# First layer input transposed on the host, its first two weight blocks side by side; the last chunks tile by tile, with smaller stores

## What is computed

```python
h = rms_norm(x, norm_mix_pre)                 # 256 x 2048
proj = h @ w_in                               # 2048 x 10240: q, k, v of two attentions, gates
q, k = rope(q), rope(k); oa, on = two attentions
mixed = sig(ga) * (oa @ w_a) + sig(gb) * (on @ w_b)
x = x + rms_norm(mixed @ w_out, norm_mix_post)
x = x + rms_norm(relu(rms_norm(x) @ w_up)**2 @ w_down, norm_mlp_post)
proj = rmsnorm(x, norm_w_2) @ w_in_2          # mLSTM and HGRN2 parts
x = x + y @ w_out_2
x = x + sigmoid(rmsnorm(x, pe_norm_w_2) @ w_pg) * (p @ w_pe)
out = rmsnorm(x, final_norm_w)
```

## Time and profile before

| | us |
|---|---|
| median of three runs (2017.31 to 2017.79) | 2017.42 |
| the profiled execution, its own time | 2017.24 |
| its span in the profile | 2015.5 |
| TensorE busy | 1992.3 (99%) |
| VectorE busy | 1175.5 (58%) |
| ScalarE busy | 981.9 (49%) |
| mean granted clock of TensorE | 0.997 |

### The profile page before, as it was taken

One profiled execution on the slowest core, in us unless ns is written; L12 is line 12 of the kernel. 1 busy time (PEld: TensorE's weight loads), 2 busy tenths in 40 slices (PEclk: granted clock), 3 DMA queues, 4 the chain that ended last, 5 costly groups with the idle time before them and its releaser, 6 DMA issues.

```text
span 2015.5 us, 22345 instructions
## 1 busy us (share of the span) xinstructions
PE 1992.3 (99%) x9256; PEld 1655.0 (82%) x9256; DVE 1175.5 (58%) x1075; ACT 981.9 (49%) x956; POOL 40.6 (2%) x42
## 2 busy tenths in 40 slices
PE   8999999999999999999999999999999999999997
PEld 6888888888888888888888888888898888888786
DVE  6645546645656644443356666677387858675554
ACT  5345544545445444444455555554556445454443
POOL 0000000000000000000000000000000000230000
PEclk9999999999999999999999999999999999999999
DMA  7564555555657356666655555564556444355442
GB/s 252 195 202 144 161 190 181 181 183 192 209 188 251 119 178 184 187 188 188 185 180 199 189 189 198 197 229 168 167 161 199 163 146 163 130 209 203 157 167 105
DMA packets 184894, 366.79 MB, mean 182 GB/s; under 512 B 6616, under 2 KB 13400, under 8 KB 184152
## 3 DMA queue, kind: packets, MB, share of 16 engines
q1 hardware_dynamic: 184792, 365.36, 55.1%
HBM read 363.24 MB, written 2.10 MB: 181 GB/s over the span
## 4 chain that ended last, share of the span: by engine, by line
PE 95%; ACT 2%; DVE 1%; issue 1%; DMA 0%; SPq 0%; POOL 0%; DVEq 0%; ACTq 0%
PE acc L1325 89%; PE mis L1325 4%; PE mis L1328 2%; ACT hi L480 1%; DVE m L844 1%; DMA raw<-in_w_in 0%; ACT ath L497 0%; DVE atl L887 0%; DVE lo L862 0%; DVE xs L844 0%; SPq L334 0%; ACT m L470 0%; ACT m L469 0%; ACT spare L480 0%; DVE m L852 0%
## 5 line engine op out<-in xcount | busy, mean ns | idle before, releaser
L862 DVE TENSOR_TENSOR lo<-raw,hi 128x2048 fp32r<-128x2048 f32 (+1 forms) x333 | 754.9, 2269 | 645.4 <-ACT hi L480 643.1
L1325 PE MATMUL acc<-hi,ath 128*128 128x512 f32 (+1 forms) x2672 | 1050.0, 393 | 4.9 <-DVE atl L887 3.8
L1325 PE MATMUL acc<-hi,atl 128*128 128x512 f32 (+1 forms) x2672 | 1034.7, 387 | 0.0
L1325 PE MATMUL acc<-lo,ath 128*128 128x512 f32 (+1 forms) x2672 | 1033.4, 387 | 0.0
L480 ACT ACTIVATE hi<-raw 128x2048 fp32r<-128x2048 f32 (+1 forms) x333 | 628.8, 1890 | 380.6 <-PE acc L1325 374.5
L1325 PEld LDWEIGHTS acc<-hi,ath 128*128 128x128 f32 x2672 | 501.9, 188 | 105.6 <-issue 5.4
L1325 PEld LDWEIGHTS acc<-hi,atl 128*128 128x128 f32 x2672 | 501.5, 188 | 102.4
L1325 PEld LDWEIGHTS acc<-lo,ath 128*128 128x128 f32 x2672 | 502.1, 188 | 98.0 <-issue 0.5
L469 ACT ACTIVATE m<-mis 128x512 f32<-128x512 f32 (+1 forms) x96 | 50.3, 524 | 222.0 <-PE mis L1328 193.1
L469 ACT ACTIVATE m<-acc,st 128x512 f32<-128x512 f32 (+1 forms) x102 | 69.3, 679 | 117.0 <-PE acc L1325 116.2
L844 DVE TENSOR_TENSOR m<-m 128x512 f32<-128x512 f32 (+2 forms) x117 | 71.9, 615 | 22.8 <-ACT m L469 18.1
(11 more groups left out here) (113 smaller groups left out, 547.4 us busy)
## 6 DMA issues: line engine op xcount, KB each, us to landing
raw<-in_w_in SPq DMA_DIRECT2D x135, 1024.0 KB, 5.1
raw<-in_w_up SPq DMA_DIRECT2D x64, 1024.0 KB, 5.5
raw<-in_w_down SPq DMA_DIRECT2D x64, 1024.0 KB, 5.0
raw<-in_w_out SPq DMA_DIRECT2D x32, 1024.0 KB, 5.1
raw<-in_w_pg SPq DMA_DIRECT2D x16, 1024.0 KB, 5.1
raw<-in_w_in SPq DMA_DIRECT2D x12, 688.0 KB, 4.2
raw<-in_w_a SPq DMA_DIRECT2D x8, 1024.0 KB, 5.1
raw<-in_w_b SPq DMA_DIRECT2D x8, 1024.0 KB, 5.0
```

Of the source, the lines that this page charges most:

```text
L862: e.tensor_tensor(lo, raw, hi.bitcast(F32), ALU.subtract).then_inc(s_lo.on("lo", n))
L1325: return e.matmul(o, a, b, start=start, stop=stop)
```

## The change

x is also given transposed from the host, as `xt` (128 partitions x 16 contraction tiles x 256 tokens), and so is p2. `XT` takes 16 KB of each partition in a region that is free at the start. The three transposes of groups on TensorE and the multiply on DVE go: ACT makes `ath` of one contraction tile for both token tiles in one ACTIVATE whose scale is the norm weight (`x_high`), DVE `atl` in one scalar_tensor_tensor (`x_low`), each of 128 x 256.

Chunks 0 to 7 are renumbered: 0, 2, 4, 6 are block 0 and 1, 3, 5, 7 block 1, so two chunks use each group of x. Chunk 1 comes in four pieces too. `first()` on TensorE takes chunk 0 piece by piece for both token tiles. ACT issues four transfers itself (`cols` and group 0 of `xt` in three) and runs a Copy of 128 x 1 on a constant ahead of its first wait. The plain x, which the row means and the residual need, comes behind chunk 5. One `warm(20, 0)` takes the place of the two runs of 12. The level masks come as bytes and are not cast.

At the end, chunks 337 to 339 are computed for t = 0 and then for t = 1. `finish` works on the last block in halves of 256 columns, the mean is folded into the squares' scale and a constant column, and a tile's rows are scaled and stored in four pieces of 384, 384, 768 and 512 columns, the second of them issued by ACT.

```diff
+        XT = m(32, 4096).rearrange("p (k s) -> p k s", k=16)
...
-        for j in range(20):
+        for j in range(2):
+            blocks.append(("rope", j, 512, []))
+        for k in range(0, 16, 4):
+            for j in range(2):
+                blocks[j][3].append(len(chunks))
+                src = w_in[k * P:(k + 4) * P, 512 * j:512 * j + 512].rearrange("(k p) c -> p k c", p=P)
+                chunks.append((src, 512, j, k, 16, "x", k))
+        for j in range(2, 20):
             kind = "rope" if j < 4 else "va" if j < 6 else "hd" if j < 10 else "vn" if j < 12 else "gt"
             plan(kind, j, w_in, 0, 16, 512 * j, 512, "x")
...
-        for j in (0, 1, 2, 3, 6, 7, 8, 9):
+        for n, j, t in ((7, 0, 0), (7, 0, 1), (8, 1, 0), (9, 1, 1)):
+            beside(n, "heads", "rope", j, t)
+        for j in (2, 3, 6, 7, 8, 9):
             for t in range(2):
                 beside(4 * j + 4 + t, "heads", "rope" if j < 4 else "hd", j, t)
...
-        beside(308, "p", 0)
-        beside(310, "p", 1)
...
-        before[0, 0] = [("x", 0, 0), ("x", 0, 1)]
-        before[0, 1] = [("x", 1, 0), ("x", 1, 1)]
-        for g in range(2, 4):
-            for t in range(2):
-                before[g - 1, t] = [("x", g, t)]
+        for g in range(1, 4):
+            behind[2 * g - 2] = [("x", g, 0)]
...
-            load(XS[:, 0, 0:512], xv[:, 0, 0:512], "x", 0, 0)
-            load(IDN[:, :], id_c, "id")
-            load(COL[:, :], cols, "col")
-            for j in range(4):
-                load(RAW[0][:, 512 * j:512 * j + 512], w_in[j * P:(j + 1) * P, 0:512], "first", j)
-                if j == 0:
-                    load(XS[:, 1, 0:512], xv[:, 1, 0:512], "x", 0, 1)
+            for n in range(2):
+                for j in range(4):
+                    load(RAW[n][:, 512 * j:512 * j + 512], w_in[j * P:(j + 1) * P, 512 * n:512 * n + 512], "first", n, j)
+            raw(2)
             for g in range(1, 4):
-                if g < 3:
-                    raw(g)
-                load(XS[:, :, 512 * g:512 * g + 512], xv[:, :, 512 * g:512 * g + 512], "x", g)
+                load(XT[:, 4 * g:4 * g + 4, :], xt_[:, 4 * g:4 * g + 4, :], "xt", g)
+                raw(2 + g)
+            for t in range(2):
+                load(XS[:, t, :], xv[:, t, :], "x", t)
             load(COS, cos_c.rearrange("(t p) c -> p t c", p=P), "cos")
             load(SIN, sin_c.rearrange("(t p) c -> p t c", p=P), "sin")
+            raw(6)
+            load(IDN[:, :], id_c, "id")
+            load(LAMV, lamv.partition_broadcast(P), "lam")
+            raw(7)
             load(NAM, nam_c, "nam")
-            load(LAMV, lamv.partition_broadcast(P), "lam")
-            load(m(24, 1024).rearrange("p (n c) -> p n c", n=8), lvl_c, "lvl")
+            load(LVL[:, :, :], lvl_c, "lvl")
             load(CAU[:, :], caus_c, "cau")
             load(BIF[:, :], bif, "bif")
-            for n in order[3:]:
+            for n in order[8:]:
...
-                    load(PN, p2.rearrange("(t p) c -> p t c", p=P), "p")
+                    load(PTT, p2.rearrange("p (k s) -> p k s", k=2), "p")
...
             for t in range(2):
-                for c in range(2):
-                    o = slice(1024 * c, 1024 * c + 1024)
-                    if c == 0:
-                        sp.wait_ge(s_act, "out", t, c)
-                    else:
-                        sp.wait_ge(s_dve, "out", t, c)
-                    e.dma_start(o_d[:, t, o], XS[:, t, o]).then_inc(s_out.on("out", t, c), 16)
+                for c in (0, 2, 3):
+                    sp.wait_ge(*((s_act if c < 2 else s_dve), "out", t, c))
+                    e.dma_start(o_d[:, t, slice(*PIECES[c])], XS[:, t, slice(*PIECES[c])]).then_inc(s_out.on("out", t, c), 16)
             sp.wait_ge(s_out, LAST)
+            sp.wait_ge(s_out2, "out", 1)
...
+                if name == "x":
+                    ac.wait_ge(loaded("xt", g), "xt", g)
+                    for k in range(4 * g, 4 * g + 4):
+                        x_high(k)
+                    return
...
+            def x_high(k):
+                ac.wait_ge(loaded("col"), "col")
+                e.activation(ATH[:, k, :], XT[:, k, :], ACT.Copy, scale=COL[:, C_PRE + k:C_PRE + k + 1]).then_inc(
+                    s_ach.on("ath", "x", k))
...
             def finish(b):
-                ids = blocks[b][3]
                 for t in range(2):
-                    ac.wait_ge(s_prod, "products", ids[-1], t)
+                    ac.wait_ge(s_prod, "products", N_ALL - 1, t)
                     ac.wait_ge(s_dve, "gated", 2, t)
-                    act(SG[t], acc[:, 2 * (b % 2) + t, :], ACT.Sigmoid, scale=ST[:, 60 + t:61 + t]).then_inc(s_act.on("evac", b, t))
-                    if t == 1:
-                        out_rows(0)
-                    ac.wait_ge(s_dve, "gated", 3, t)
-                    act(JK2, XS[:, t, 1536:2048], ACT.Square, accum=ST[:, 43 + 4 * t:44 + 4 * t]).then_inc(s_act.on("out sq", 3, t))
-                out_rows(1)
-
-            def out_rows(t):
-                ac.wait_ge(s_pool, "row", N_ALL - 1, t)
-                ac.wait_ge(s_dve, "weighed", 1, t)
-                act(XS[:, t, 0:1024], XS[:, t, 0:1024], ACT.Copy, scale=ST[:, 48 + t:49 + t]).then_inc(s_act.on("out", t, 0))
-
-            do = dict(lam=lam, da=da, na=na, sig=sig, ut=ut, cut=cut, prep=prep, conv=conv, gate=gate, hg=hg, ml=ml, p=p)
+                    for h in range(2):
+                        o = slice(256 * h, 256 * h + 256)
+                        act(SG[t][:, o], acc[:, 2 * (b % 2) + t, o], ACT.Sigmoid, scale=ST[:, 60 + t:61 + t]).then_inc(
+                            s_act.on("last sigmoid", t, h))
+                    for h in range(2):
+                        ac.wait_ge(s_dve, "gated", 3, t, h)
+                        act(JK2[:, 0:256], XS[:, t, 1536 + 256 * h:1792 + 256 * h], ACT.Square, scale=D ** -0.5,
+                            accum=SUMS[t][:, 3 + h:4 + h]).then_inc(s_act.on("last sq", t, h))
+                    for c in range(2):
+                        o = slice(*PIECES[c])
+                        ac.wait_ge(s_pool, "row", N_ALL - 1, t)
+                        ac.wait_ge(s_dve, "weighed", 1, t)
+                        act(XS[:, t, o], XS[:, t, o], ACT.Copy, scale=ST[:, 48 + t:49 + t]).then_inc(s_act.on("out", t, c))
...
-            unit("x", 0, 0)
-            first(0)
-            unit("x", 0, 1)
-            for j in range(1, 4):
-                first(j)
-            high(1)
+            def first(n, j):
+                h, w = (z[n][:, 512 * j:512 * j + 512] for z in (HI, RAW))
+                ac.wait_ge(loaded("first", n, j), "first", n, j)
+                e.activation(h, w, ACT.Copy).then_inc(s_hi.on("hi first", n, j))
+
+            e.dma_start(COL[:, :], cols).then_inc(loaded("col").on("col"), 16)
+            for k, c in ((0, 1), (1, 1), (2, 2)):
+                e.dma_start(XT[:, k:k + c, :], xt_[:, k:k + c, :]).then_inc(loaded("xt", 0, k).on("xt", 0, k), 16)
+            ac.wait_ge(s_pool, "mhalf")
+            act(MHALF[:, 15:16], MHALF[:, 15:16], ACT.Copy).then_inc(s_act.on("table"))
+            for j in range(4):
+                ac.wait_ge(loaded("xt", 0, min(j, 2)), "xt", 0, min(j, 2))
+                x_high(j)
+                first(0, j)
+            for j in range(4):
+                first(1, j)
...
-                if n == 3:
+                if n == 4:
                     for t in range(2):
-                        for g in range(4):
-                            ac.wait_ge(loaded(*(("x", 0, t) if g == 0 else ("x", g))), *(("x", 0, t) if g == 0 else ("x", g)))
+                        ac.wait_ge(loaded("x", t), "x", t)
                         act(m(48, 2048), XS[:, t, :], ACT.Square, accum=ST[:, t:t + 1]).then_inc(s_act.on("x sq", t))
...
+            def x_low(k):
+                dv.wait_ge(s_ach, "ath", "x", k)
+                e.scalar_tensor_tensor(ATL[:, k, :], XT[:, k, :], COL[:, C_PRE + k:C_PRE + k + 1], ATH[:, k, :].bitcast(F32),
+                                       ALU.mult, ALU.subtract).then_inc(s_dve.on("atl", "x", k))
+
+            def first(n, j):
+                h, l, w = (z[n][:, 512 * j:512 * j + 512] for z in (HI, LO, RAW))
+                dv.wait_ge(s_hi, "hi first", n, j)
+                e.tensor_tensor(l, w, h.bitcast(F32), ALU.subtract).then_inc(s_lo.on(*(("lo first", n, j) if j < 3 else ("lo", n))))
...
             def finish(b):
-                gated(3, 0, b)
-                row_mean(N_ALL - 1, 0, None)
-                gated(3, 1, b)
-                weighed(3, 0)
-                row_mean(N_ALL - 1, 1, None)
-                out_rows(0)
-                weighed(3, 1)
-                out_rows(1)
+                for t in range(2):
+                    r = ST[:, 48 + t:49 + t]
+                    for h in range(2):
+                        x_, g_ = XS[:, t, 1536 + 256 * h:1792 + 256 * h], SG[t][:, 256 * h:256 * h + 256]
```

(52 more changed lines are left out.)

92 lines of the change are left out of this document (33 added, 59 removed).

## The result

Measured four times beside the kernel before, the changed kernel takes **2006.42 us** in the median (2006.01 to 2007.72) against 2017.39 (2017.31 to 2017.79): a ratio of 0.9946, with a 95% interval of 0.9929 to 0.9964. That is 11.0 us gained where 8.9 were forecast. The profiled execution took 2006.48, with a span of 2004.6 us.

The account below looks back on a forecast made before the run. TensorE, busy 1992.3 of 2015.5 us, was taken as the bound. Start 8.0 + p2 0.0 - chunk 338 0.1 + end 1.0 = 8.9 off 2017.24 gave 2008.3, median 2008.5; range 2004.5 to 2012.5.

Parts of the forecast that it names:

- Chunk 2: At the start: lands at 15.5, is copied, subtracted, waits for four `x_low`; starts at 21.75, TensorE idle 2.85 us.
- The pace: TensorE at the start: chunks 2 to 7 take 5.48 us each.
- The rotary step: Block 0's step on DVE: 2.55 us a token tile, done at 56.0; TensorE waits 1.0 us before chunk 8.
- the yardstick: Last transposes of block 1's rotary step, in turn 9: at 67.9 against 75.88 before, 8.0 us gained.
- p2: Its four transposes go, some 0.4 us of TensorE, but TensorE reaches the same wait for `atl` earlier: 0 gained.
- Chunk 338: Near the end: its `lo` is done at 1991.6, just when the new order needs it; up to 0.1 us lost.
- The end: After the last matmul: last stores' bytes run from 2010.85 to 2013.5 instead of until 2014.6; 1.0 us gained.
- The clock falls: Rival, 12%: TensorE's wait before chunk 2 brings half clock, costing 1.7 us; 2009.3, at worst 2011.
- Half given back: Rival, 18%: thin margins on ACT and DVE at the start cost 3 to 4 us of waits; 2012.
- chunk 6 starves: Rival, 5%: chunk 6, behind 2 MB of plain x, lands at 52.0 rather than 36.4; 2024.
- No effect: Rival, 4%: `xt` lands too late for an earlier first product; only transposes saved, about 3 us with the end; 2014.5.
- The start is fed faster or waits less: Rival, 18%: two issuing queues land chunks 2 and 6 up to 3 us earlier; 2.4 us more gained, 2006.

Follow-up runs that it names:

- e3: Changed kernel with `cols` and group 0 of `xt` issued by SP between chunk 0's pieces, nothing issued by ACT: 2008.23 us.
- e5: Changed kernel with the old end: last chunks in pairs, finish in whole blocks, four stores of 512 KB: 2007.65 us, ratio 0.9952.
- e6: Kernel before the change with only the new finish, stores and order of the last chunks: 2016.48 us, ratio 0.9996.
- e4: Changed kernel with chunk 2 also in four pieces, group 1 of `xt` loaded and split ahead of it: 2007.27 us.
- e7: Changed kernel with block 0 first and then block 1, so that chunk 1 comes whole: 2012.15 us, ratio 0.9974.

## Why the prediction was right, and by what it was off

**Sign and mechanism: right; the two waits at the start were sized wrong.** The gain is won ahead of turn 9 and carried to the end (10.1 there, 9.8 at the last matmul), with the forecast chain, and a last microsecond at the end. Of the signs named in advance, the first product (6.77, asked for 6.5 to 8), the wait of 1.6 at p2 and the 8.2 us between the two tiles' last steps (DVE's at 1991.80 and 1999.95) came true. The wait for `x_low` before chunk 2 (1.47, asked for 2 to 3.5), the wait near 1 for the rotary step (none) and turn 9 near 68 (65.80) did not.

**Chunk 2** was to land at 15.5 and start at 21.75; it was 14.73 and 20.70. The arrival was 0.8 too late, because I kept the rate of the old early stretches (144 to 219 GB/s) in the anchor of 12.99, while the new one moves 294 where 219 were moved. This is the rival in which the start is fed faster. The Trainium skill's rule that I cited beside it ("DMA: Bandwidth & Descriptors", Issuing engines are not separate DMA queues) says that a second queue saves issue time only, and no row here contradicts it. But what is saved early on was worth something: 157 GB/s with one queue and 197 with two, so the conclusion that the sum stays did not follow. e3, the changed kernel with one queue, lands chunk 2 at 15.07 and chunk 6 at 36.31, where the forecast had 15.5 and 36.4. The four `x_low` took 1.67, not 1.95: that was 0.28 of the bound by the nearest row. The wait before chunk 2, forecast 2.85, was 1.47 by its row: the start came 1.05 earlier, chunk 1 ended 0.2 later, and the row counts from the last matmul's modelled end.

**The pace.** From 20.70 to 53.47 six chunks took 5.46 each, I had 5.48: 0.1.

**The rotary step** is where the rest went. Its length was right (48.77 to 53.86, 5.09 against 2 x 2.55), but it was to end at 56.0 and TensorE to wait 1.0. It ended 2.1 earlier, 1.4 of it because chunk 6 came at 35.03 and not at 36.4, the rest in small steps of ACT and DVE (four `x_high` took 1.69 there, not 1.9), and TensorE arrived at the same moment. With 1.05 (chunk 2), 1.0 (this wait) and 0.1 (pace) the 2.1 between 67.9 and 65.80 are accounted for on TensorE's side. On the other side the forecast put the yardstick 31.5 behind the landing of chunk 6, and it stands 30.8 behind it: 1.4 by the landing and 0.7 by the small steps. The table shows how near it was: in every run with a wait there Y follows those transposes by 11.89 to 11.92, whatever happened at the start. The two limits lay within a microsecond of each other. That the second wait was 0 in the profiled execution and not 0.8 is partly chance: e5 has the same start, and there chunk 2 landed 0.6 earlier, chunk 6 0.35 later, and TensorE waited 0.78. The forecast's "wait of 2.85, then 1.0" was the right picture with both waits too long.

**p2** 0, as forecast, and its wait is the 1.6 foretold. **Chunk 338** and all else behind p2: 10.06 - 9.80 = 0.26 lost, 0.1 forecast; e6 shows the same loss (94.98 against 94.70), so it belongs to the new order of the last chunks. **The end** +1.0, measured 1.0 to 1.1 in the traces. The last stores moved 357 GB/s in a stretch that holds their start and end: 1.04 MB in 2.9 us, where 2.7 were forecast, so the smaller pieces cost at most 0.2. The Trainium skill's table ("DMA: Bandwidth & Descriptors", Bandwidth), by which I worked out 240 GB/s and 1.7 us more, did not fit this case. It is a table of loads from HBM to SBUF issued from GpSimd, one size to a row, and these are stores from SP and ACT that follow each other on the queues.

**The rivals.** *The clock falls* did not happen in the profiled execution, but it was closer than 12% sounds: e3, e4 and e7 all show it, once. *Half given back* and *chunk 6 starves*: no wait from 21 to 66 at all; 398 GB/s in 11.50 to 27.00. *No effect*: out. *The start is fed faster or waits less*, to which I gave 18%, named 2006, and the measured 2006.42 lies nearer to that than to 2008.5: its condition, chunks 2 and 6 landing earlier, came true by 0.8 and 1.4 us out of its up to 3. The second queue, put at nothing in the sum, is most of what the forecast was off by, as far as one execution of e3 tells.
